# Dense networks: three pairs of steps by seven block products, with VectorE's sums and low parts in another order

## The reference

```python
def swiglu(x, w_gate, w_up, w_down):
    return (jax.nn.silu(x @ w_gate) * (x @ w_up)) @ w_down
...
        h = h + 0.5 * swiglu(rms_norm_2(h, ffn_norm[layer, 0]), ffn_w_gate[layer, 0], ffn_w_up[layer, 0], ffn_w_down[layer, 0])
```

## Time and profile before

| | |
|---|---|
| runs (3), median | 2225.48 us (2225.2 to 2225.76) |
| profiled execution | 2225.49 us, span 2223.6 us |
| TensorE, VectorE, ScalarE busy over the span | 2086.9, 1190.4, 808.0 us |
| TensorE busy in network 0 | 181.43 of 181.50 us |
| in network 1 | 177.74 of 178.20 us |
| in network 2 | 177.72 of 178.20 us |
| in network 3 | 177.19 of 177.30 us |

### The profile page before, as it was taken

One profiled execution on the slowest core, in us unless ns is written; L12 is line 12 of the kernel. 1 busy time (PEld: TensorE's weight loads), 2 busy tenths in 40 slices (PEclk: granted clock), 3 DMA queues, 4 the chain that ended last, 5 costly groups with the idle time before them and its releaser, 6 DMA issues.

```text
span 2223.6 us, 27395 instructions
## 1 busy us (share of the span) xinstructions
PE 2086.9 (94%) x10956; PEld 1279.9 (58%) x10956; DVE 1190.4 (54%) x1785; ACT 808.0 (36%) x1263; POOL 28.1 (1%) x38
## 2 busy tenths in 40 slices
PE   5999999999999899889976999999999999989998
PEld 3447743333333333323322888778888888867887
DVE  6976612222222222222214877677886886685976
ACT  6045321121111111101102555565555554375544
POOL 0000000000000000000000000100000000200000
PEclk8999989999999999999998999999999999999999
DMA  7782799999999999999999452327445443414451
GB/s 325 267 319 105 274 420 416 415 426 427 427 428 427 427 428 428 427 426 428 428 426 410 195 227 113 119 102 286 191 159 205 169 171 136 167 44 174 186 211 45
DMA packets 49845, 633.85 MB, mean 285 GB/s; under 512 B 5809, under 2 KB 5809, under 8 KB 6993
## 3 DMA queue, kind: packets, MB, share of 16 engines
q1 hardware_dynamic: 49712, 632.04, 69.3%
HBM read 630.97 MB, written 1.05 MB: 284 GB/s over the span
## 4 chain that ended last, share of the span: by engine, by line
PE 74%; DMA 16%; DVE 4%; ACT 4%; issue 1%; SPq 0%; DVEq 0%; ACTq 0%
DMA piece<-in_moe 16%; PE bank L2429 13%; PE bank L2306 13%; PE bank L2308 13%; PE bank L2307 13%; PE bank L2470 6%; PE bank L2404 3%; PE bank L2494 2%; PE bank L1059 2%; PE bank L2948 1%; PE bank L3018 1%; PE bank L746 1%; PE bank L372 1%; PE bank L2445 1%; DVE prob_n L1302 1%
## 5 line engine op out<-in xcount | busy, mean ns | idle before, releaser
L2429 PE MATMUL bank<-piece,xeT 128*64 128x512 f32 (+1 forms) x2304 | 445.0, 613 | 53.2 <-DMA piece<-in_moe 45.2
L2312 DVE TENSOR_TENSOR ffn_lo<-slot,ffn_hi 128x2048 fp32r<-128x2048 f32 x148 | 337.7, 2289 | 100.1 <-ACT ffn_hi L3272 99.6
L3272 ACT ACTIVATE ffn_hi<-slot 128x2048 fp32r<-128x2048 f32 x148 | 281.7, 1914 | 119.0 <-PE bank L2308 107.0
L2429 PEld LDWEIGHTS bank<-piece,xeT 128*64 128x64 f32 (+1 forms) x2304 | 134.1, 130 | 330.0 <-issue 305.6
L2550 DVE TENSOR_TENSOR hT<-hT,bank 128x512 f32<-128x512 f32 x144 | 92.2, 682 | 257.9 <-PE bank L2494 257.8
L2306 PE MATMUL bank<-ffn_hi,hT_hi 128*128 128x512 f32 x512 | 202.3, 395 | 0.0
L2308 PE MATMUL bank<-ffn_hi,hT_lo 128*128 128x512 f32 x512 | 199.7, 390 | 0.0
L2307 PE MATMUL bank<-ffn_lo,hT_hi 128*128 128x512 f32 x512 | 199.4, 389 | 0.0
L2599 DVE TENSOR_SCALAR work<-bank 128x256 f32<-128x256 f32 x60 | 25.5, 425 | 323.5 <-PE bank L2438 323.5
L2662 ACT ACTIVATE work<-bank 128x256 f32<-128x256 f32 x30 | 11.5, 384 | 289.6 <-PE bank L2445 289.6
L2308 PE MATMUL bank<-ffn_hi,act_lo 128*128 128x512 f32 x288 | 114.3, 397 | 0.0
(11 more groups left out here) (789 smaller groups left out, 3257.3 us busy)
## 6 DMA issues: line engine op xcount, KB each, us to landing
piece<-in_moe SPq DMA_DIRECT2D x190, 2048.0 KB, 25.9
slot<-in_ffn SPq DMA_DIRECT2D x44, 2048.0 KB, 8.1
slot<-in_ffn SPq DMA_DIRECT2D x44, 1024.0 KB, 7.9
slot<-in_ada SPq DMA_DIRECT2D x16, 1024.0 KB, 5.3
slot<-in_nsa_in SPq DMA_DIRECT2D x5, 2048.0 KB, 8.5
slot<-in_merge SPq DMA_DIRECT2D x3, 3072.0 KB, 12.8
slot<-in_ada SPq DMA_DIRECT2D x2, 3072.0 KB, 18.8
slot<-in_w_in SPq DMA_DIRECT2D x6, 1024.0 KB, 7.8
```

The lines of the kernel that those rows point to most:

```text
L2312: return dve.tensor_tensor(lo, x, hi.bitcast(F32), ALU.subtract)
L2429: mm = pe.matmul(bank[n * c:n * (c + 1), :], x[:, kt, :], w[i][:, at:at + 512], start=kt == 0, stop=False)
L3272: act.activation(k["ffn_hi"][:, room, :], ffn_plain(k, q, what), ACT.Copy).then_inc(s["ffn_down_hi"] if isinstance(what, int) else s["ffn_ ...
```

## The change

Pairs stand at steps 3, 6 and 9, so three per network, with one plain step after each of the first two and five plain steps in all. T1 no longer has a place of its own: T3 = B22 - B12, T2 = T3 + B11, T1 = B22 - T2 are written over weight blocks, T3 ahead of the pair, the others behind the low parts that still need those blocks. The rooms, the order of the loads, and the orders of conversions at a network's start and end change with it.

```diff
-FFN_PAIRS = (4, 8)
-FFN_DOWNS = (0, 1, 2, 3, 5, 4, 6, 7, 9, 8, 10)
+FFN_PAIRS = (3, 6, 9)
+FFN_DOWNS = (0, 1, 2, 4, 3, 5, 7, 6, 8, 10, 9)
...
-DOWN_ROOM = {0: 3, 1: 2, 2: 3, 3: 3, 5: 2, 4: 3, 6: 2, 7: 2, 9: 3, 8: 2, 10: 3}
+DOWN_ROOM = {0: 2, 1: 2, 2: 2, 4: 3, 3: 2, 5: 2, 7: 3, 6: 2, 8: 2, 10: 1, 9: 3}
...
+FFN_LOADS = [(what, m) for what, group in (("both", (0, 1, 2)), ("down", (0, 1, 2)), ("both", (3, 4, 5)), ("down", (3, 4))) for m in group]
...
-PAIR_SUMS = ("T1", "T3", "T2", "T4")
+PAIR_SUMS = ("T3", "T2", "T1", "T4")
...
     def pair(m):
         low(m, "A11 B11")
-        pair_landed(m)
-        pair_sum(m, "T1")
-        turned_low(m - 2)
-        pair_sum(m, "T3")
-        low(m, "S4 B22")
         pair_sum(m, "T2")
+        low(m, "S4 B22")
+        pair_sum(m, "T1")
         swiglu(m - 1)
         low(m, "A12 B21")
         pair_sum(m, "T4")
-        low(m - 1)
+        if between is not None or last:
+            low(m - 1)
         low(m, "S2 T2")
         turned_low(m - 1)
...
         low(m, "A22 T4")
+        if between is None and not last:
+            low(m - 1)
...
     ffn_norm_scalar(k, act, i, gain, 1)
+    high(0)
     high(1, 0)
     stream_squares_scalar(k, act, i)
     act.wait_ge(s["xn_ready"], 2 * i + 2)
     high(1, 1)
     silu(0)
-    high(0)
     turned_high(0)
...
     if q == 1:
         ffn_weights_high(k, act, 2, 0, 0)
-    silu(FFN_LAST)
+    turned_high(FFN_DOWNS[-1])
     if q == 1:
         ffn_weights_high(k, act, 2, 0, 1)
```

More of the change, by code:

```diff
@@ L2779, in ffn_turns @@
         down(m - 1)
-        plain(m + 2, 0)
+        if m + 2 < FFN_STEPS:
+            plain(m + 2, 0)
         down(m + 1)
-        plain(m + 2, 1)
+        if m + 2 < FFN_STEPS:
+            plain(m + 2, 1)
         down(m)
[L2784 to L2787, removed]
     return forms, turns
@@ L3180, in join, with first_sum, pair @@
         ins.then_inc(s["ffn_joined"], 1)
-    def pair(m):
+    def first_sum(m):
+        pair_landed(m)
+        pair_sum(m, "T3")
+    def pair(m, between=None):
+        last = m + 2 == FFN_STEPS
         low(m, "A11 B11")
-        pair_landed(m)
+        if between is not None:
+            between()
+        pair_sum(m, "T2")
+        low(m, "S4 B22")
         pair_sum(m, "T1")
-        turned_low(m - 2)
-        pair_sum(m, "T3")
-        low(m, "S4 B22")
-        pair_sum(m, "T2")
         swiglu(m - 1)
@@ L3199, in pair @@
         low(m, "A22 T4")
+        if between is None and not last:
+            low(m - 1)
         for name in PAIR_JOINS[1:5]:
             join(m, name)
-        low(m + 2, 0)
+        if not last:
+            low(m + 2, 0)
         swiglu(m + 1)
@@ L3206, in pair @@
         low(m + 1)
[L3207 to L3210, removed]
+        if last:
+            turned_low(m + 1)
+            low(m)
+        else:
+            turned_low(m + 1)
+            low(m + 2, 1)
+            turned_low(m)
+            low(m)
+            first_sum(m + 3)
     i = FFN_NORM[q]
@@ L3216, in ffn_vector @@
     ffn_norm_vector(k, dve, i, gain, 1)
+    low(0)
     low(1, 0)
@@ L3312, in keep, with pair @@
         act.activation(k["behind"][:, 2048 + 512 * n:2560 + 512 * n], pair_banks(k, q, m)[bank], ACT.Copy).then_inc(s["ffn_kept"], 1)
-    def pair(m):
+    def pair(m, between=None):
+        last = m + 2 == FFN_STEPS
         high(m, "A11 B11")
-        turned_high(m - 2)
+        if between is not None:
+            between()
         high(m, "S4 B22")
@@ L3319, in pair @@
         high(m, "A12 B21")
-        high(m - 1)
+        if between is not None or last:
+            high(m - 1)
         keep(m, 0)
@@ L3327, in pair @@
         high(m, "A22 T4")
-        high(m + 2, 0)
+        if between is None and not last:
+            high(m - 1)
+        if not last:
+            high(m + 2, 0)
+        else:
+            high(m + 1)
         silu(m + 1)
         silu(m)
-        high(m + 1)
+        if not last:
+            high(m + 1)
         turned_high(m + 1)
-        high(m + 2, 1)
-        high(m)
-        turned_high(m)
+        if last:
+            high(m)
+        else:
+            high(m + 2, 1)
+            turned_high(m)
+            high(m)
     i = FFN_NORM[q]
@@ L3346, in ffn_scalar @@
     silu(0)
-    high(0)
     turned_high(0)
     high(2, 0)
-    high(1)
+    sums_high()
     silu(1)
     high(2, 1)
[L3353 to L3365, removed]
+    high(1)
+    pair(FFN_PAIRS[0], lambda: turned_high(1))
+    for m in FFN_PAIRS[1:]:
+        pair(m)
     if q == 1:
         ffn_weights_high(k, act, 2, 0, 0)
-    silu(FFN_LAST)
+    turned_high(FFN_DOWNS[-1])
     if q == 1:
@@ L3372, in ffn_scalar @@
         following()
-    turned_high(FFN_LAST)
 def final_scalar(k, act):
```

98 lines of the change are left out of this document (42 added, 56 removed).

## The result

The changed kernel takes 2244.57 us (median of 4 runs, 2243.88 to 2244.85) against 2225.62 for the kernel before (4 runs): 1.0083 times as long [1.0065, 1.01], 19.0 us. The forecast was 2237 in a range up to 2244: the sign and the places were right, the price was 7.6 us too low, which puts the time 0.6 us above the range.

What follows compares the result with a forecast made beforehand. TensorE's own matmuls were taken to bound the kernel, busy 94% of the span. 2225.5 - 10.9 (matmuls) + 12.2 + 0.8 (starts, clock) + 8.2 (pairs) + 1.6 (end of network 1) = 2237 us, range 2228 to 2244.

Steps and rivals of the forecast that it cites:

- Term 1: One more pair in each of four networks removes 48 matmuls from TensorE: -10.9 us.
- Term 2: Start of networks 1 and 3: (1,0) waits behind down(0)'s late rows, +12.2 us, and a slowed clock, +0.8 us.
- I take 0.4 us each time: Start of networks 1 and 3: loss from TensorE's slow clock on (1,0) after each gap, +0.8 us together.
- about 1 us in which TensorE would wait for VectorE anyway: Behind (1,0)'s matmuls in networks 1 and 3: a wait said to hide about 1 of 1.7 us lost to the clock.
- so the landing does not move against the network: Start of networks 1 and 3: SyncE's first six loads keep their order, so down(0)'s rows land at the same relative time.
- The 2245 that the prediction gives for that case: Networks 1 and 3: both (1,0) half steps slow throughout by the clock rule alone, total near 2245 us.
- Term 3: Pairs: VectorE's chain of sums makes TensorE wait in each network's last pair, 2.05 us a network, +8.2 us.
- rival (d): VectorE becomes the bound in every pair, with waits in 8 more pairs: 2241 to 2245 us; chance 0.16.
- at the end down(10) waits some 0.2 us: End of each network: down(10) waits some 0.2 us for the low part of its turned rows, behind a pair.
- Term 4: End of network 1: network 2's low part of (0,1) delays the additions to x before the transposes, +1.6 us.
- Rival (a): Start of networks 1 and 3: the down rows are there in time, total 2224.4 us; chance 0.08.
- rival (b): Last pair does not wait because VectorE's chain runs 1.8 us faster: 2230 us or a little less; chance 0.12.

Runs made afterwards that it cites:

- e_pair_end: e_all with VectorE's work at the end of the last pair reordered to use its idle time ahead of the gating products; 2216.49 us, 0.9958 of before.
- e_load_order: The changed kernel with down(0)'s rows loaded right after step 0's own weights, ahead of those of steps 1 and 2; 2229.74 us, 1.0019 of before.
- e_before_down0_first: The kernel before with only down(0) converted ahead of (1,0) on both engines, pairs, loads and rooms as before; 2238.8 us, 1.006 of before.
- e_fill_gap: The changed kernel with 24 extra unused matmuls behind (0,1) in each of networks 1 and 3, filling TensorE's gaps; 2240.68 us.
- e_act_buffers: The changed kernel with step 10's turned rows in the second pair of buffers and step 9's in the first; 2241.95 us.
- e_tail: The changed kernel with the low part of network 2's (0,1) moved from the end of network 1 into network 2; 2241.89 us.
- e_last_low: The changed kernel with the last pair's conversions of step 8's down rows put behind those of A22 T4 on both engines; 2241.61 us.
- e_all: The changed kernel with the four edits of e_load_order, e_last_low, e_act_buffers and e_tail together; 2223.13 us, 0.999 of before.
- e_down0_back: The changed kernel with down(0)'s conversions put back behind step 0's gating on ScalarE and VectorE, loads as changed; 2247.3 us.

## Why the forecast was right in its direction and too low

**Term 1, right.** 48 matmuls went, and once nothing waits they are worth nearly what was said: e_pair_end is 9.8 us under the kernel before beside it, of -10.9.

**Term 2, right mechanism, too small.** 13.0 forecast, 16.4 measured; e_load_order gives back 14.8 by moving nothing but the load, and e_before_down0_first brings 13.5 by itself. Two steps failed. The first is "I take 0.4 us each time": (1,0) ran 1.76 and 2.88 us longer, since the clock fell before the matmuls began and stayed down well into them. Of the "about 1 us in which TensorE would wait for VectorE anyway", 0.7 was there each time (VectorE's gating was through 1.1 and 2.3 us before the transposes), so by e_fill_gap the clock cost 1.0 + 2.2 = 3.2, not 0.8. The second is "so the landing does not move against the network": in network 3 ScalarE began on the rows 11.84 us after the network's start, where the forecast's 2044.5 is 10.4, 1.5 us more. In network 1 the landing was as forecast, and with the 12.70 us of e_fill_gap the wait comes to 6.1 us, not 6.6. (Network 2's load is issued 13.4 us before its first matmul, at 1676.88, and not 16; it is there in time either way.) The rule of the Trainium skill that the prediction weighed ("TensorE: Matmul & The Clock Gate", Part 1: idleness gates the array to half its clock, sustained activity releases it) agrees with e_fill_gap, where matmuls alone kept the clock at 1.00; taken as two half steps slow throughout it would have cost too much, since (1,0) needed 7.20 and 8.32 us and not 10.9. The 2245 that the prediction gives for that case still has the hidden 1 us in it; without it the sum is 2247.

**Term 3, one part right, one step wrong.** The wait of "1.7 to 1.8 us" for S2 T2 in the last pair measured 1.62 in each network, 1.78 from start to start, and first and middle pairs had none, so rival (d), VectorE the bound in every pair, did not happen. The step "at the end down(10) waits some 0.2 us" failed: it waited 1.13, 1.33 from start to start. I counted VectorE's queue and not who may write `act_hi`: down(10) now follows down(8), both use that buffer, and only four transposes stand between their products, where the other pairs have a half step there as well. e_act_buffers takes the wait away by the buffer alone. The term was 8.2 and measured 12.4.

**Term 4, right in its place, its size in part by luck.** 1.6 forecast for the wait for x (its own terms, 4.4 + 0.6 + 0.7, give 1.5), 1.0 measured from start to start, by the low part named (e_tail). The other 0.6, at down(9), was not forecast, and e_tail leaves it; its cause was not tested.

Together 3.4 (term 2) + 4.2 (term 3) make up the 7.6 us missed. Rival (a) failed at the landing, as argued against it, and rival (b) at the measured 1.62.

My theory on the last pair needed mending on the way: the two waits are not separate. Each edit alone leaves 1.62 (e_act_buffers) or 1.69 us (e_last_low) a network in the last pair, and both together (e_all) still leave 1.69. What ended both was using VectorE's idle time under the silus, beside the free buffer.

## What to carry to other kernels

When a conversion moves forward in a queue, move its load with it: an engine that works in order passes a late landing on to everything behind it. When the order of products changes, list who writes and who reads every shared buffer in the new order, not only the queues. Where one edit takes a wait away and the time hardly moves, look for the same microseconds further on, and for idle time on the engine that is late, before calling it the bound.

## What the hardware did that was not expected

A gap of 2.57 us (e_down0_back) was followed by a clock of 0.50 in networks 0, 1 and 3, but of 1.00 behind the same gap in network 2; behind the 1.62 and 1.13 us gaps of the changed kernel it was 1.00 in all four networks. Behind the 1.62 of network 0:

```profile
1368.00:1371.40 3.40, 3.40 (x15) 2.69 (x16) 3.40 (x3) 0.68 (x2) 0.00 (x0) 1.00 0.00 0
```

So gaps of some 2.6 us were followed by 1.4 us of lost matmul time in three networks, and by none in the fourth. And 48 matmuls added to idle stretches made the kernel 3.9 us faster, of which 3.2 us can be put down to the clock.
